# Fourier layer: tokens folded twice ahead of the transforms, and the channel transform moved ahead of the last block of z

## What is computed

```python
def fourier_mixer(h, w_in, w_mix, b_mix, w_out):
    u, z = jnp.split(h @ w_in, 2, axis=-1)
    ug = u.reshape(b_, t, 8, 128)
    f = jnp.fft.fftn(ug, axes=(1, 3), norm="ortho").real
    f = jnp.einsum('btgc,gce->btge', f, w_mix).reshape(b_, t, 1024) + b_mix
    return (f * jax.nn.silu(z)) @ w_out
```

## Time and profile before

| | |
|---|---|
| median of 3 executions | 2535.53 us (2534.56 to 2537.11) |
| the profiled execution, its own time | 2540.85 us |
| its span | 2539.0 us |
| mean granted TensorE clock | 0.969 of full speed |
| PE matmul busy | 2309.0 us, 91% of the span |
| DVE busy, ACT busy, POOL busy | 1140.9 (45%), 780.4 (31%), 623.8 (25%) us |
| the Fourier block (start to about 519 us) | PE busy 493.8 of 519.2 us |

### The profile page before, as it was taken

How to read it: one execution, slowest core, us unless ns; L and a number is a source line. 1 busy time by engine, 2 the same in 40 slices (tenths; PEclk the granted TensorE clock), 3 DMA queues, 4 the chain that set the end, 5 groups by cost and what they waited for, 6 DMA issues and landing times. The chain is left out here.

```text
span 2539.0 us, 56698 instructions
## 1 busy us (share of the span) xinstructions
PE 2309.0 (91%) x24172; PEld 1455.8 (57%) x24172; DVE 1140.9 (45%) x2235; ACT 780.4 (31%) x1992; POOL 623.8 (25%) x913
## 2 busy tenths in 40 slices
PE   7999999999969997999997798989899898988598
PEld 3555555534534443544443677777777777777354
DVE  4111111112374675021220566666666666665684
ACT  4000000013314551220000344444444444454221
POOL 0000000001212331000000444444454444443243
PEclk9999999999979998999999799999999999999699
DMA  9200000150002765455422234333333333331542
GB/s 366 118 17 25 17 21 21 67 199 25 34 35 72 200 191 157 146 153 172 166 91 88 76 94 149 88 92 88 91 83 95 83 92 85 91 88 49 189 125 87
DMA packets 296667, 261.95 MB, mean 103 GB/s; under 512 B 105440, under 2 KB 255200, under 8 KB 293856
## 3 DMA queue, kind: packets, MB, share of 16 engines
q1 hardware_dynamic: 296416, 258.32, 32.9%
HBM read 178.54 MB, written 79.69 MB: 102 GB/s over the span
## 5 line engine op out<-in xcount | busy, mean ns | idle before, releaser
L770 PE MATMUL ps<-xt,w_slab 128*128 128x512 f32 (+1 forms) x1376 | 551.4, 557 | 28.8 <-DMA w_slab<-in_w 18.9
L770 PEld LDWEIGHTS ps<-xt,w_slab 128*128 128x128 f32 x1376 | 260.3, 192 | 315.2 <-issue 263.6
L363 PE MATMUL ps<-h,fw_slab 128*128 128x512 f32 (+1 forms) x768 | 278.1, 524 | 2.1 <-ACT h L250 2.1
L1676 PE MATMUL ps<-M,AT 64*64 64x64 f32 x6400 | 270.9, 224 | 4.8 <-DVE M L1576 2.0
L1439 POOL TENSOR_TENSOR SP<-Q,decay 64x128 f32<-64x128 f32 x304 | 138.1, 454 | 464.1 <-DVE Q L1616 434.9
L1676 PEld LDWEIGHTS ps<-M,AT 64*64 64x64 f32 x6400 | 220.0, 135 | 48.4 <-issue 14.6
L1676 PE MATMUL ps<-TT,MT 64*64 64x64 f32 x5120 | 216.8, 224 | 18.5 <-ACT XT L1501 15.3
L363 PEld LDWEIGHTS ps<-h,fw_slab 128*128 128x128 f32 x768 | 146.4, 191 | 132.4 <-issue 124.1
L1676 PEld LDWEIGHTS ps<-TT,MT 64*64 64x64 f32 x5120 | 178.2, 135 | 49.4 <-issue 38.2
L1562 DVE COPY_PREDICATED TT<-mask,ps 128x256 f32<-128x256 int32 x400 | 166.8, 435 | 75.9 <-PE ps L1676 73.1
L532 POOL TENSOR_TENSOR xt<-scaled_out,xt 128x1024 f32<-128x1024 f32 x10 | 23.5, 2348 | 666.2 <-DVE scaled_out L565 666.2
(11 more groups left out here) (195 smaller groups left out, 3101.0 us busy)
## 6 DMA issues: line engine op xcount, KB each, us to landing
feat<-feature_scratch SPq DMA_DIRECT2D x160, 256.0 KB, 3.0
feature_scratch<-k_feats SPq DMA_DIRECT2D x64, 320.0 KB, 5.1
w_slab<-in_rwin SPq DMA_DIRECT2D x32, 512.0 KB, 5.9
feature_scratch<-k_feats SPq DMA_DIRECT2D x24, 640.0 KB, 6.9
mod_slab<-in_modw SPq DMA_DIRECT2D x8, 1536.0 KB, 6.6
Q<-v_token_scratch SPq DMA_DIRECT2D x320, 32.0 KB, 2.5
Z<-v_token_scratch SPq DMA_DIRECT2D x320, 32.0 KB, 2.3
fgo<-in_modw SPq DMA_DIRECT2D x8, 1024.0 KB, 9.7
```

The lines of the kernel that those rows point to most:

```text
L363: mm = pe.matmul(ps[:, b0 + b, 0:n], wi[:, half, k, :], h0[:, k, a:a + n], start=k == 0, stop=k == KT - 1)
L770: mm = pe.matmul(ps[:, bank, 0:n], w[:, i % 2, k, :], src[:, k, a:a + n], start=k == 0, stop=k == KT - 1)
L1676: mm = pe.matmul(out[o, b, :], L[o, b, :], R[o, b, :], start=True, stop=True)
```

## The change

Both transforms over tokens use their symmetry before the matmuls, no longer only after them.

1. **First fold.** DVE adds and subtracts token t and token N - t: for the latent part into `ue` and `uo` (512 columns each, read once forward and once in reversed order), for the context into the two halves of `uc`. `ub` has two more columns, which hold zero, so that the partner of token 0 is zero.
2. **Second fold.** DVE adds and subtracts token t and 512 - t of `ue` and of `uo`, into the four parts of `uq` (256 columns each). Even output tokens take two of the parts and odd ones the other two, a cosine and a sine part each.
3. **Channel transform** (`channels(g)`): eight matmuls of 128 columns for `uq`, two for `uc`, and two with a single column as weights for the columns that have no partner (column 256 of `ue`, context token 128), into one partition of bank 0. It stands between block 1 and block 2 of z. DVE copies banks 6 and 7 into `ab`, ACT copies bank 0 into `ab` and `am`.
4. **Token transform** (`time_parts`): four banks (sine even, sine odd, cosine even, cosine odd), two matmuls each of 257 or 256 columns, one more with a single contraction row (`am` against `tm`) for the middle tokens, then the context: two matmuls of 256 columns and one with a single contraction row.
5. **Recombining.** DVE writes even and odd output tokens with a step of two, forward and reversed (four operations of 256 columns), after two copies by ACT.
6. The tables shrink from 4.6 MB to 1.3 MB. Three memsets of one column on DVE stand ahead of the copy of the modulation rows. The gate's turn in group 0 stands behind the four banks, and the context matmuls of group 0 wait for `gate_done`.

The core of the diff (eight leading blanks are left out in each line):

```diff
+    QUART, U0 = HALF // 2, CTX + 1
...
-    tl = sb("time_tab_lat", [P, KT, 2, HALF])
-    alt = sb("alt", [P, 2])
-    tc = sb("time_tab_ctx", [P, 2, 2, CTX])
-    ub = sb("u_group", [P, T])
+    te = sb("time_tab_even", [P, 2, 2, QUART + 1])
+    to = sb("time_tab_odd", [P, 2, 2, QUART])
+    tc = sb("time_tab_ctx", [P, 2, CTX])
+    tm = sb("time_tab_mid", [1, QUART + 1 + CTX])
+    ub = sb("u_group", [P, T + 2])
+    ue, uo = sb("u_even", [P, HALF + 1]), sb("u_odd", [P, HALF + 1])
+    work = sb("fold_work", [P, 2 * T])
     zb = sb("z_group", [P, 1, T])
-    ab = sb("ab_group", [P, NCH, 2 * P])
-    qs = sb("q_part", [P, HALF])
+    am = sb("mid_rows", [1, 2 * P])
+    qs = sb("q_part", [P, 2 * QUART + 1])
     fb = sb("f_group", [P, T])
...
+    sq = work[:].rearrange("p (s t) -> p s t", s=2)
+    ab = work[:, 0:T].rearrange("p (c e) -> p c e", c=NCH)
+    uq = work[:, T:T + 4 * QUART].rearrange("p (s t) -> p s t", s=4)
+    uc = work[:, T + 4 * QUART:2 * T].rearrange("p (s t) -> p s t", s=2)
+    rstd, rows, grows = ub[:, 0:T], qs[:, 0:512], fb
+    zeros, fold1, fold2, abx_out = sem("u_zeros"), sem("u_folded_once"), sem("u_folded_twice"), sem("ab_ctx_out")
...
-            sp.dma_start(tl[:], A["tlat"]).then_inc(tl_in, 16)
-            sp.dma_start(alt[:], A["alt"]).then_inc(tl_in, 16)
+            sp.dma_start(te[:], A["teven"]).then_inc(tl_in, 16)
+            sp.dma_start(to[:], A["todd"]).then_inc(tl_in, 16)
+            sp.dma_start(tm[:], A["tmid"]).then_inc(tl_in, 16)
             sp.dma_start(tc[:], A["tctx"]).then_inc(tl_in, 16)
...
-                for b, (a, n) in enumerate(BLK):
+                if g:
+                    act.wait_ge(fold1, g * 5)
+                    act.wait_ge(ab_mm, g * 3)
+                act.wait_ge(u_mm, g * 3 + 1)
+                act.activation(ub[:, 0:CTX], ps[:, 0, 0:CTX], ACT.Copy).then_inc(u_out, 1)
+                act.activation(ub[:, U0:U0 + 512 - CTX], ps[:, 0, CTX:512], ACT.Copy).then_inc(u_out, 1)
+                for b in (1, 2):
+                    a, n = BLK[b]
                     act.wait_ge(u_mm, g * 3 + (b + 1))
-                    if b == 0 and g:
-                        act.wait_ge(ab_mm, g * 5)
-                    act.activation(ub[:, a:a + n], ps[:, b, 0:n], ACT.Copy).then_inc(u_out, 1)
+                    act.activation(ub[:, a + 1:a + 1 + n], ps[:, b, 0:n], ACT.Copy).then_inc(u_out, 1)
+                act.activation(ue[:, HALF:HALF + 1], ps[:, 1, CTX:CTX + 1], ACT.Copy).then_inc(u_out, 1)
...
                     act.activation(zsig[:, a:a + n], ps[:, 3 + b, 0:n], ACT.Sigmoid).then_inc(zs_out, 1)
-                act.wait_ge(f_mm, g * 3 + 2)
-                act.activation(qs[:], ps[:, 4, :], ACT.Copy).then_inc(q_out, 1)
+                    if b == 1:
+                        act.wait_ge(ab_mm, g * 3 + 3)
+                        act.activation(ab[:, 8:10, :], ps[:, 0, 0:2 * P].rearrange("p (c e) -> p c e", c=2), ACT.Copy).then_inc(abx_out, 1)
+                        act.activation(am[:], ps[0:1, 0, 2 * P:4 * P], ACT.Copy).then_inc(abx_out, 1)
+                act.wait_ge(f_mm, g * 5 + 1)
+                act.activation(qs[:, 0:QUART + 1], ps[:, 6, 0:QUART + 1], ACT.Copy).then_inc(q_out, 1)
+                act.wait_ge(f_mm, g * 5 + 2)
+                act.activation(qs[:, QUART + 1:2 * QUART + 1], ps[:, 7, 0:QUART], ACT.Copy).then_inc(q_out, 1)
...
+            v.wait_ge(xn_ready, KT)
+            for z in (ub[:, CTX:CTX + 1], ub[:, T + 1:T + 2], uo[:, HALF:HALF + 1]):
+                v.memset(z, 0.0).then_inc(zeros, 1)
...
+                lo, hi = ub[:, U0:U0 + HALF], ub[:, U0 + HALF + 1:T + 2][:, ::-1]
+                v.wait_ge(u_out, g * 5 + 5)
+                if g == 0:
+                    v.wait_ge(zeros, 3)
+                v.tensor_tensor(ue[:, 0:HALF], lo, hi, ALU.add).then_inc(fold1, 1)
+                v.tensor_tensor(uo[:, 1:HALF], lo[:, 1:], hi[:, 1:], ALU.subtract).then_inc(fold1, 1)
+                v.tensor_tensor(uo[:, 0:1], lo[:, QUART:QUART + 1], hi[:, QUART:QUART + 1], ALU.subtract).then_inc(fold1, 1)
+                for i, op in enumerate((ALU.add, ALU.subtract)):
+                    v.tensor_tensor(uc[:, i, :], ub[:, 0:P], ub[:, P + 1:CTX + 1][:, ::-1], op).then_inc(fold1, 1)
+                v.wait_ge(fold1, g * 5 + 3)
+                for i, (u, op) in enumerate(((ue, ALU.add), (ue, ALU.subtract), (uo, ALU.subtract), (uo, ALU.add))):
+                    v.tensor_tensor(uq[:, i, :], u[:, 0:QUART], u[:, QUART + 1:HALF + 1][:, ::-1], op).then_inc(fold2, 1)
                 for b, (a, n) in enumerate(BLK):
+                    if b == 2:
+                        for q in range(2):
+                            v.wait_ge(ab_mm, g * 3 + q + 1)
+                            v.tensor_copy(ab[:, 4 * q:4 * q + 4, :], ps[:, 6 + q, :].rearrange("p (c e) -> p c e", c=4)).then_inc(ab_out, 1)
                     v.wait_ge(zs_out, g * 3 + (b + 1))
...
-                for q in range(NCH // 2):
-                    v.wait_ge(ab_mm, g * 5 + (q + 1))
-                    v.tensor_copy(ab[:, 2 * q:2 * q + 2, :], ps[:, (6 + q) % 8, :].rearrange("p (t e) -> p t e", t=2)).then_inc(ab_out, 1)
...
-                v.wait_ge(f_mm, g * 3 + 3)
+                L = CTX + HALF
+                v.wait_ge(f_mm, g * 5 + 3)
+                v.wait_ge(q_out, g * 2 + 1)
+                v.tensor_tensor(fb[:, CTX:L:2], ps[:, 3, 0:QUART], qs[:, 0:QUART], ALU.subtract).then_inc(f_out, 1)
+                v.tensor_tensor(fb[:, L:T:2][:, ::-1], ps[:, 3, 1:QUART + 1], qs[:, 1:QUART + 1], ALU.add).then_inc(f_out, 1)
+                v.wait_ge(f_mm, g * 5 + 4)
+                v.wait_ge(q_out, g * 2 + 2)
+                v.tensor_tensor(fb[:, CTX + 1:L:2], ps[:, 4, 0:QUART], qs[:, QUART + 1:2 * QUART + 1], ALU.subtract).then_inc(f_out, 1)
+                v.tensor_tensor(fb[:, L + 1:T:2][:, ::-1], ps[:, 4, 0:QUART], qs[:, QUART + 1:2 * QUART + 1], ALU.add).then_inc(f_out, 1)
+                v.wait_ge(f_mm, g * 5 + 5)
                 v.tensor_copy(fb[:, 0:CTX], ps[:, 5, 0:CTX]).then_inc(f_out, 1)
-                v.tensor_copy(fb[:, CTX + HALF:CTX + HALF + 1], ps[:, 5, CTX:CTX + 1]).then_inc(f_out, 1)
-                v.wait_ge(q_out, g + 1)
-                v.tensor_tensor(fb[:, CTX:CTX + HALF], ps[:, 3, :], qs[:], ALU.subtract).then_inc(f_out, 1)
-                v.tensor_tensor(fb[:, CTX + HALF + 1:T][:, ::-1], ps[:, 3, 1:HALF], qs[:, 1:HALF], ALU.add).then_inc(f_out, 1)
-                v.wait_ge(f_out, g * 4 + 4)
+                v.wait_ge(f_out, g * 5 + 5)
...
+
+            def channels(g):
+
+                pe.wait_ge(fold2, g * 4 + 4)
+                pe.wait_ge(fold1, g * 5 + 5)
+                for q in range(2):
+                    if g == 0 and q == 1:
+                        pe.wait_ge(mod_done, 2)
+                    for i in range(4):
+                        mm = pe.matmul(ps[:, 6 + q, i * P:i * P + P], uq[:, 2 * q + i // 2, i % 2 * P:i % 2 * P + P],
+                                       cw[:, g, q * P:q * P + P], start=True, stop=True)
+                    mm.then_inc(ab_mm, 1)
+                for c in range(2):
+                    pe.matmul(ps[:, 0, c * P:c * P + P], uc[:, c, :], cw[:, g, c * P:c * P + P], start=True, stop=True)
+                for i, u in enumerate((ue[:, QUART:QUART + 1], ub[:, P:P + 1])):
+                    mm = pe.matmul(ps[0:1, 0, (2 + i) * P:(3 + i) * P], u, cw[:, g, 0:P], start=True, stop=True)
+                mm.then_inc(ab_mm, 1)
+
+            def time_parts(bank, first, tab, mid=False):
+                n = tab.shape[2]
+                for q in range(2):
+                    mm = pe.matmul(ps[:, bank, 0:n], ab[:, first + q, :], tab[:, q, :], start=q == 0, stop=q == 1 and not mid)
+                if mid:
+                    mm = pe.matmul(ps[:, bank, 0:n], am[:, 0:P], tm[:, 0:n], start=False, stop=True)
+                mm.then_inc(f_mm, 1)
...
                     pe.wait_ge(win, g * 16 + 16)
-                    if g:
-                        pe.wait_ge(*((f_out, g * 4) if half else (ab_out, g * 5)))
-                    elif half == 0:
+                    if g and half:
+                        pe.wait_ge(f_out, g * 5)
+                    elif g == 0 and half == 0:
                         pe.wait_ge(cwr, KT)
                     for b, (a, n) in enumerate(BLK):
+                        if half and b == 2:
+                            channels(g)
...
-                pe.wait_ge(u_out, g * 3 + 3)
...
-                for q in range(NCH // 2):
-                    if g == 0 and q == 1:
-                        pe.wait_ge(mod_done, 2)
-                    if g == 0 and q == 3:
-                        pe.wait_ge(gate_rows, 1)
-                    for t in range(2):
-                        mm = pe.matmul(ps[:, (6 + q) % 8, t * 256:t * 256 + 256], ub[:, (2 * q + t) * P:(2 * q + t + 1) * P],
-                                       cw[:, g, :], start=True, stop=True)
```

(49 more changed lines are left out.)

## The result

The changed kernel takes 2430.26 us (median; 2424.90 to 2431.31) where the kernel before takes 2536.32 beside it: the ratio is estimated as 0.9574, with a 95% interval of 0.9550 to 0.9598. Timed a second time it was 2429.42 beside 2540.42, ratio 0.9571 (0.9558 to 0.9584). That is 106 and 111 us less. (The four executions of the kernel before in the first timing hold one of 2559.86 us; the other three are those of the table ahead of the prediction, and against their median of 2535.53 it is 105 us less.) The forecast was 111.5 us less and 2424 us, with a range of 2409 to 2440.

What follows compares the result with a forecast made beforehand. TensorE (PE), busy 91% of the span, bounds the kernel. Savings of 97.6 us (groups 1 to 7), 12.8 (group 0) and 1.3, minus 0.2, make 111.5; 2535.5 - 111.5 = 2424 us, range 2409 to 2434, chance 0.80 (2440 with a rival's part).

Steps and rivals of the forecast that it cites:

- Part 1: Channel transform: 5.35 us a group removed, 24 passes of 128 columns added at 2.69 us.
- the rates: PE time per pass from the earlier trace: 0.430 us for 512 columns, 0.215 for 256, 0.112 for 128.
- rival of weight loads in the open: Small passes can't hide their weight loads, so 128-column passes take twice 0.112: 21.5 us in all, 2446; chance 0.03.
- Part 2: Token transform: 17.32 us a group removed, 24 passes of 256 columns added at 5.16; single-row passes cost their columns.
- rival of slow passes on the new tables: Token transform: odd table starts double the time of 6 passes, 10 us in all, 2434, or 2445; chance 0.10.
- Part 3, switches: PE leaving full-width passes for single-column or single-row ones and returning: 3 x 0.29 = 0.87 us a group.
- Part 4, waits: PE's waits in the new order: the 0.88 us wait goes, none replaces it; 3.2 us fold under 12.95 us cover.
- Group 0: First group: 12.8 us less, after adding 0.60 for the gate rows' turn and 0.7 for the gate_done wait.
- the edges: Block end: 1.3 us less as DVE operations come earlier; ahead of the loop: 0.2 us more for three memsets.
- the load of the output weights: Loaded when z ends, landing 12.2 us later; projection 16 us after the load, cover 4 us: cost 0 to 2 us.
- a chain of 30 us: DVE's fold comes so late that PE stands before the channel transform: 26 us slower, 2560; chance 0.03 for slower.
- Single passes at no cost: Single-column and single-row passes of both transforms could be free: up to 8 us less in all.

Runs made afterwards that it cites:

- half-change: Changed kernel with the first fold only, two token-transform banks of 512 columns, latent output token 512 left out: 2459.24 us, 47.13 us a group.
- left-out passes: Changed kernel without the four single-row passes of each group, so the output lacks the middle tokens' share: 2416.55 us, 41.65 us a group.
- passes over 128 rows: Changed kernel with the four single-row passes contracting over 128 rows, 127 of them zero: 2420.43 us, ratio to before 0.9539, 42.52 us a group.
- fillers: Changed kernel plus unread matmuls around the modulation rows' turn, behind the last group and at the next block's start: 2421.06 us, ratio to before 0.9539.
- run with twelve additions: Changed kernel with twelve extra unread DVE additions of 1280 columns between the two folds of each group: 2518.94 us, first such group 53.55 us.

## Why the prediction was right

**The bound.** PE was the bound and stayed it: no row of group 1 has an idle time. The half-change and the left-out passes moved the period by their passes, to 0.1 us.

**Part 1 and the rates.** 24 passes of 128 columns were priced at 2.69 us and took 2.85 with their switches. The rate of 0.112 from the earlier trace rows held with weights in `uq` (1.79 for 16). So the rival of weight loads in the open is out, and with it the rule of the Trainium skill quoted there (TensorE: Matmul & The Clock Gate, Part 3) for such passes.

**Part 2.** 24 passes at 0.215 us: 5.16 forecast, 5.87 less the gaps of 0.7 measured. A pass over one row costs its columns, as taken. The rival of slow passes on the new tables is out: 257 columns from an odd start took 0.87 us for four.

**Part 3, switches.** Forecast 0.87 us a group with 0.29 for each excursion, by the two-column passes of the earlier trace rows. Measured 0.39 for each of the two single-row ones, by both the left-out passes and those over 128 rows, and 0.28 for the single-column one, by the rows of group 1. With the single-row ones gone, 42.52 - 34.38 - 2.69 - 5.16 = 0.29 is left, which is the same. So the 0.29 held for the column kind, from which it was taken, and was 0.10 too low for the row kind, for which the prediction had no row. Twice 0.10 is the whole difference between 43.10 and 43.30. Both kinds cost, as the rule quoted there (TensorEngine Tiling, Key Properties) has it.

**Part 4, waits.** None in groups 1 to 7. The fold was priced at 3.2 us and took 3.1, the cover at 12.95 and was 13.05 (123.69 to 136.74). Moving the channel transform was worth 0.86 us a group: moved back, a wait of 0.82 us for ACT's copies stands where the 0.88 of the earlier trace rows stood.

**Group 0 and the edges.** The wait for gate_done was 0.33 us and not 0.7. The memsets cost nothing that shows: the copy behind them begins within 0.1 us of the end of the normalisation, as in the kernel before. Here the mis-sized term is the clock. I counted an unchanged cost for the low clock at u's first passes and at the next block's, and in the first profiled execution it was 1.4 us more in the one (u and z of group 0 take 37.7 us after 36.2) and 0.7 in the other. At the next block the idle time fell from 6.0 to 4.8 us, as forecast, but the eight passes behind it took 6.26 us instead of 5.56, and in the other executions without fillers 5.0 to 6.2.

**The 6 us between 2424 and 2430.** For the profiled execution the forecast was 2429.3 and 2431.3 was measured; the period and group 0 are 1.4 us each above their terms, the edges 1.4 together, and the unchanged rest 2.2 below. The period's 1.4 is the row kind of switch and group 0's 1.4 is the clock. The rest came in when I took 111.5 us from a median of three executions, 5.3 us below the profiled one. Before's median was 2535.5 with three executions and 2539 to 2540 in the two larger sets of later timings, so against those the same gain gives 2428 to 2429. The weak step is that conversion. Two profiled executions of the changed kernel differ by 7.9 us, of which 3.1 are the clock in group 0 and 3.4 lie in the unchanged stretch, and a median of three doesn't remove such differences. That the forecast still lay within 6 us is in part luck: the unchanged rest was 2.2 us shorter, and the prediction had put it at nothing.

**Slips in the working.** Before, the projection came 34.25 us after the load of the output weights, not 34.4. A chain of 30 us would cost 8 x 17.05 - 111.5 = 25 us and not 26, and the 2 us a group for the clock, named there, are not in it; the run with twelve additions paid them. Single passes at no cost would save 8 x 1.26 = 10 us and not 8. None of them changes the forecast.

Still open: why the fillers lowered the median by 8 to 9 us where 5.8 are seen in their places, and the passes over 128 rows by 9 to 10 where 6.2 are. The profiles give no sign that the fillers' effect lasts into the unchanged stretch: with them it took 2008.1 and 2010.6 us, without them 2006.1 to 2011.9.

## What to carry to other kernels

Where TensorE has no idle time in a stretch, count passes by their columns at the rate of the nearest rows, and the period comes out to 1%; folding inputs by symmetry on an idle engine pays in full as long as it ends within its cover, which two rows give. Keep every matmul of such a loop in one shape: here a contraction over one row was 0.39 us cheaper over 128 rows of which 127 are zero. Compare a forecast with executions of the same kind (profiled with profiled), since executions of one kernel differed by 8 us here, and the median of three of the kernel before by 4 to 5 from those of larger sets.

## What the runs showed of the hardware

- Single-row passes between full-width ones cost 0.39 us an excursion, single-column ones 0.28, beside their columns.
- After 8.3 us of idle time the 16 passes of 128 columns took 3.57 us instead of 1.79, at a granted clock of 0.50. After the same 2.1 us wait in two executions of one kernel (and 1.9 and 1.2 us of idle time a little earlier), the clock fell in one and not in the other: 3.1 us of group 0.
- With two to four filler passes ahead of and behind a wait, no idle time longer than 1.2 us was left there, and the clock stayed at 1.00, in both profiled kernels that had them.
- DVE reads SBUF backwards at the forward rate: 0.69 us for 512 columns, as z's product of 512 forward, and writes with a step of two in 0.41 to 0.43 us for 256, like the plain copy.
